# Second layer's entry in a two-layer decoder kernel: the overflow branch, three idle products, waits by depth half, and the bank of the first query projection

## The reference

```python
for i in range(DEPTH):
    if i % 2 == 0:
        mix = moba_attention(x, moba_w_in[j], moba_w_out[j], rel_bias)
    else:
        mix = nsa_attention(x, nsa_w_in[j], nsa_w_out[j], ..., rel_bias)
    x = layer_norm(DEEPNORM_ALPHA * x + mix, ln_g[i, 0], ln_b[i, 0])
    ffn = grouped_moe(x, router_w, router_b, moe_w_gate[i], moe_w_up[i], moe_w_down[i])
    x = layer_norm(DEEPNORM_ALPHA * x + ffn, ln_g[i, 1], ln_b[i, 1])

def nsa_attention(x, w_in, ...):
    proj = x @ w_in
    sizes = [H * d] + [Hkv * d] * 6 + [3 * H]
    q, kc, vc, ks, vs, kw, vw, g = jnp.split(proj, np.cumsum(sizes)[:-1].tolist(), axis=-1)
```

## Time and profile before

| | |
|---|---|
| median of 3 runs | 1209.3 us (1207.87 to 1209.31) |
| the profiled execution's own time | 1207.55 us |
| its span, first to last instruction | 1205.7 us |
| mean granted TensorE clock | 0.935 |
| PE busy | 1021.0 us, 85% of the span |
| DVE, ACT busy | 310.5 us, 183.4 us |
| chain that ended last | PE 52%, DMA 42%, DVE 2%, ACT 1%, issue 1% |
| HBM read | 446.72 MB |

### The profile page before, as it was taken

How to read it: one execution, slowest core, us unless ns; L and a number is a source line. 1 busy time by engine, 2 the same in 40 slices (tenths; PEclk the granted TensorE clock), 3 DMA queues, 4 the chain that set the end, 5 groups by cost and what they waited for, 6 DMA issues and landing times.

```text
span 1205.7 us, 18281 instructions
## 1 busy us (share of the span) xinstructions
PE 1021.0 (85%) x7610; PEld 565.5 (47%) x7610; DVE 310.5 (26%) x866; ACT 183.4 (15%) x473; POOL 43.3 (4%) x109
## 2 busy tenths in 40 slices
PE   9999999976698975668899999999967798876766
PEld 7586544443343532343678655544523433432432
DVE  2435521321111111111221785403211111111112
ACT  1024210110010000000221563201100010100002
POOL 1001010000000000000100120100000000000000
PEclk9999999998899988889999999999987899978888
DMA  9955899999999999999995308999999999999995
GB/s 354 364 210 192 341 373 418 427 427 427 427 428 428 426 425 429 428 428 422 368 352 214 137 1 316 357 422 425 426 427 428 426 426 428 428 426 428 427 426 236
DMA packets 56851, 449.05 MB, mean 372 GB/s; under 512 B 4643, under 2 KB 11044, under 8 KB 29628
## 3 DMA queue, kind: packets, MB, share of 16 engines
q1 hardware_dynamic: 54752, 442.52, 89.1%
q0 software_dynamic: 1680, 4.88, 1.1%
q10 hardware_dynamic: 332, 0.42, 0.1%
HBM read 446.72 MB, written 1.07 MB: 371 GB/s over the span
## 4 chain that ended last, share of the span: by engine, by line
PE 52%; DMA 42%; DVE 2%; ACT 1%; issue 1%; SPq 1%; DVEq 0%
DMA ring<-in_moe_w_down 16%; PE bank L1010 14%; DMA ring<-in_moe_w_up 11%; DMA ring<-in_moe_w_gate 10%; PE bank L779 7%; DMA bias<-in_moe_w_up 5%; PE bank L857 4%; PE bank L968 4%; PE bank L1074 3%; PE bank L1050 2%; PE bank L1224 2%; PE bank L1089 2%; PE bank L1331 1%; PE bank L1321 1%; PE bank L1061 1%; PE bank L1250 1%
## 5 line engine op out<-in xcount | busy, mean ns | idle before, releaser
L1010 PE MATMUL bank<-ring,work 128*32 128x256 f32 (+1 forms) x2656 | 323.6, 473 | 106.6 <-DMA ring<-in_moe_w_up 36.8
L1010 PEld LDWEIGHTS bank<-ring,work 128*32 128x32 f32 (+1 forms) x2656 | 151.9, 130 | 233.1 <-issue 201.8
L1635 DVE TENSOR_TENSOR work<-work,bank 128x256 f32<-128x256 f32 (+1 forms) x32 | 15.6, 487 | 526.0 <-PE bank L1010 526.0
L1074 PE MATMUL bank<-ring,work 128*32 128x512 f32 x576 | 99.3, 658 | 13.0 <-DMA ring<-in_moe_w_down 8.0
L1010 PE MATMUL bank<-softmax_area,work 128*32 128x256 f32 (+1 forms) x352 | 65.3, 499 | 32.8 <-DMA ring<-in_moe_w_gate 22.2
L779 PE MATMUL bank<-xT,ring 128*128 128x256 f32 x384 | 85.7, 382 | 1.1 <-ACT acc L482 1.1
L1648 DVE TENSOR_TENSOR xs<-xs,bank 128x512 f32<-128x512 f32 x112 | 71.0, 682 | 41.4 <-PE bank L1092 23.2
L779 PEld LDWEIGHTS bank<-xT,ring 128*128 128x128 f32 x384 | 72.1, 190 | 13.3 <-issue 3.8
L1010 PE MATMUL bank<-bias,work 128*32 128x256 f32 (+1 forms) x384 | 77.6, 485 | 0.0
L968 PE MATMUL bank<-work,acc 128*128 128x128 f32 (+1 forms) x448 | 75.5, 323 | 0.0
L968 PEld LDWEIGHTS bank<-work,acc 128*128 128x128 f32 x448 | 66.0, 191 | 16.6 <-issue 11.5
(11 more groups left out here) (286 smaller groups left out, 1128.3 us busy)
## 6 DMA issues: line engine op xcount, KB each, us to landing
ring<-in_moe_w_gate SPq DMA_DIRECT2D x44, 2048.0 KB, 28.7
ring<-in_moe_w_up SPq DMA_DIRECT2D x40, 2048.0 KB, 30.0
ring<-in_moe_w_down SPq DMA_DIRECT2D x36, 2048.0 KB, 29.2
softmax_area<-in_moe_w_down SPq DMA_DIRECT2D x8, 2048.0 KB, 25.8
bias<-in_moe_w_gate SPq DMA_DIRECT2D x6, 2048.0 KB, 33.1
softmax_area<-in_moe_w_up SPq DMA_DIRECT2D x6, 2048.0 KB, 28.5
bias<-in_moe_w_up SPq DMA_DIRECT2D x6, 2048.0 KB, 28.8
bias<-in_moe_w_down SPq DMA_DIRECT2D x6, 2048.0 KB, 33.3
```

The costliest lines, as they stand in the source:

```text
L1010: last = mm(bank[2 + k][row:row + cap, 0:width], xgT_of(group_of[i])[:, t, at + e * cap:at + (e + 1) * cap], w[e](t)[:, part * width:(part ...
L1074: last = mm(bank[5][row:row + CAP_NARROW, :], hidT_narrow[:, m, CAP_NARROW * e:CAP_NARROW * (e + 1)], w[e](m)[:, n * 512:(n + 1) * 512], s ...
```

## The change

Four edits, all at the second layer's entry. The four idle products at the end of `experts(0)` go; three stand instead behind `overflow(0)`, ahead of the wait for tile 0. `first_tiles` takes its products by depth half, each half with a wait of its own for the copy of that half; the wait for both halves goes. With it, a bank's start flag is set on its first product only, and its stop flag on its last. The first query projection (g = 3) is written to bank 5 and does not wait for bank 1, and ACT reads it there.

```diff
+        FIRST_QUERY_BANK = 5
...
             def project_T(l, g, w, lhs_cols, free=False):
 
+                b = FIRST_QUERY_BANK if l == 1 and g == 3 else g % 2
                 if not free:
                     proj_bank_free(l, g)
                 for n, pick_cols in enumerate(lhs_cols):
                     for t in range(KT):
-                        last = mm(bank[g % 2][:, n * SEQ:(n + 1) * SEQ], pick_cols(w, t), xT[:, t, :],
+                        last = mm(bank[b][:, n * SEQ:(n + 1) * SEQ], pick_cols(w, t), xT[:, t, :],
                                   start=(t == 0), stop=(t == KT - 1))
...
                 spread(l, PAIRS - 1)
-                if l + 1 < LAYERS:
-                    keep_warm(4)
...
-                    last = project_T(1, g, w, [tile_cols(2 * part), tile_cols(2 * part + 1)], free=(g == 4))
+                    last = project_T(1, g, w, [tile_cols(2 * part), tile_cols(2 * part + 1)], free=g in (3, 4))
...
             def first_tiles(tt, g):
                 w = nsa_slot(slot8, 0)
-                for n in range(2):
-                    for t in range(KT):
-                        last = mm(bank[g][:, n * SEQ + tt * P:n * SEQ + (tt + 1) * P], tile_cols(2 * g + n)(w, t),
-                                  xT[:, t, tt * P:(tt + 1) * P], start=(t == 0), stop=(t == KT - 1))
+                for half in range(2):
+                    pe.wait_ge(xT_copied, 2 * (2 * NT + tt) + half + 1)
+                    for n in range(2):
+                        for t in range(KT // 2 * half, KT // 2 * (half + 1)):
+                            last = mm(bank[g][:, n * SEQ + tt * P:n * SEQ + (tt + 1) * P], tile_cols(2 * g + n)(w, t),
+                                      xT[:, t, tt * P:(tt + 1) * P], start=tt == n == t == 0, stop=tt == n == 1 and t == KT - 1)
                 return last
 
+            keep_warm(3)
             normed(0, 1, 0)
             transpose_x(2, 0)
             arrived(1, 0)
-            xT_here(2, 0)
             first_tiles(0, 0)
             normed(0, 1, 1)
             transpose_x(2, 1)
             first_tiles(0, 1)
-            xT_here(2, 1)
...
-                    last = s_.mul(qT[:, 4 * c:4 * c + 2, :].rearrange("p m q -> p (m q)"), bank[1][:, :], DH ** -0.5)
+                    last = s_.mul(qT[:, 4 * c:4 * c + 2, :].rearrange("p m q -> p (m q)"), bank[FIRST_QUERY_BANK if g == 3 else 1][:, :], DH ** -0.5)
```

## The result

The changed kernel took 1211.51 us (median of 12 runs, 1209.51 to 1213.9), the kernel before 1209.37 us (12 runs, 1207.8 to 1211.89). The ratio is 1.0020, with a 95% interval of 1.0011 to 1.0029: slower by 1.3 to 3.5 us. The forecast was 1210.5 us in a range of 1207.1 to 1212.2.

A forecast was written before the change was run, and what follows sets the result against it. It took PE's work and waits between the layers as the bound, passed on one to one. +2.0 +1.3 -0.54 -0.45 -1.05 = +1.26, say +1.2 us, took 1209.3 to 1210.5 us; range 1207.1 to 1212.2.

The forecast's parts named there:

- my forecast proper: Second layer's entry: code fetched late, one spell of lower clock; +0.5 to +2.0 us, 1209.8 to 1211.3 us, chance 0.57.
- the slower rival: Behind layer 0's branch: code at 587.35 as now, two lower-clock spells; +3.4 us, 1212.7 us, chance 0.14.
- Code behind the branch: After layer 0's overflow branch: fetched code arrives at 586.7 us, the three products follow it, first transposes 2.0 us later.
- Clock: Behind 3.9 us of idle PE after the last expert sum: lower granted clock costs 1.3 us, bounds nothing and 2.74.
- Half waits: First projection of the second layer: starts after the first of two ACT copies, winning 0.54 us.
- Stall: Wait inside the first projection at 592.90 us: the second page of code comes in time, winning 0.45 us.
- Bank 5: First query projection: no longer waits for ACT's bank 1 copies, starts at 607.53 instead of 608.59 us, winning 1.05 us.
- Sum: Shift at the first query projection, passed on one to one: +2.0 +1.3 -0.54 -0.45 -1.05 = +1.26 us.
- the cheap branch: Layer 0's branch costs only 0.94 us: -2.5 to -2.95 us, 1206.4 to 1206.8 us; chance 0.17 for over 2.4 us gain.
- the kept clock: Rival behind layer 0's branch: fetch exposed but no clock loss, sum about -0.1 us, 1209.2 us, chance 0.12.

The follow-up runs named there:

- both_covers: The changed kernel with four idle products put back ahead of the branch, three kept behind it; 1209.91 us, ratio to the kernel before 1.0004.
- branch_only: The kernel before with only the idle products changed: none ahead of the overflow branch, three behind it; 1212.94 us, ratio 1.0033.
- halves_bank5: The changed kernel's depth-half waits and bank 5, with the four idle products ahead of the branch as before; 1208.84 us, ratio 0.9995.
- no_branch: halves_bank5 with TensorE's branch and overflow body of layer 0 left out; 1205.91 us, ratio to the kernel before 0.9978.

## Why the prediction came out as it did

The time lay in the range and on the forecast side, and the mechanism was the forecast one. Its size was too small: +1.26 us in the sum, +1.86 in the trace and +2.1 in the medians. The 1211.51 us lie just above the band of my forecast proper (1209.8 to 1211.3), toward the slower rival. By its steps:

- **Code behind the branch.** Right in kind: it is fetched, the products were its cover, and moved behind it they cover nothing. The size was off. I put the code at 586.7, 5.9 us after the spread's start, because I took the fetch to start sooner without products ahead of the branch. It did not: its packet started 3.7 us after the spread's start, as before. The code came at 6.46, and at 6.41 to 6.63 in every kernel whose branch stands behind the last spread. With the three products at the higher clock level that makes 2.58 us (4.28 less the clock's 1.70) where I had 2.0. Why that packet starts 3.7 us after the spread's start, and only 1.0 us after it at the end of layer 1 (1195.7 against 1194.71 in the earlier trace rows), no run shows. I put it down to the full transfer queues; that was not tested.
- **Clock.** Predicted 1.3, measured 1.70 (the changed kernel against both_covers); in branch_only 2.6 (5.28 against 2.68). The lower level came in all four kernels with 4.4 us and more of idle PE at this place. It lasted about 3.4 us in the changed kernel, but twice that in the other three (6.6 us and more at 0.50), in branch_only behind the same idle time of 4.47 us. So the single spell was in part luck: the length of the idle stretch, by which I had chosen it, does not decide it. With the 2.6 us of branch_only the sum would be +2.8 us. The upper value of "0.55 to 0.63" in the prediction stands in none of its rows.
- **Half waits.** Predicted 0.54; from the first transpose to the projection it is 1.36 us against 1.94, so 0.58. What I had not seen is a condition: where the first projection runs into the second piece of code, as in halves_bank5, the wait for that piece eats this gain.
- **Stall.** Predicted gone, 0.45 won. It is gone, and the block is 0.71 us shorter (3.65 against 4.36), which is more than the idle time of PE alone; before, the weight loads had stood still for 0.64 us there.
- **Bank 5.** Predicted 1.05, measured 1.13 (0.22 us from the start of L1350 to that of the query product, against 1.35).
- **Sum.** +4.28 -0.58 -0.71 -1.13 = +1.86 us at the query product. Both losses were larger than I had put them (by 0.58 and 0.40 us), and the three gains together by 0.38 us, so the errors partly cancel. Nothing behind the query product took it up or added to it beyond the noise: from its start to the span's end it is 597.1 us before and 597.3 after.

Of the rivals, the cheap branch is excluded by the 4.47 us of "issue" and the kept clock by PEclk. The slower one (code as late as now, two spells) was right on the code, and branch_only shows two spells. The changed kernel has a trace of one execution only; how many spells its other runs had, up to 1213.9 us, is not known.

## What to carry to other kernels

In this kernel a taken branch over a long body cost the engine a fetch, not a jump. Idle products that keep the clock belong ahead of such a branch; useful work should serve as well, which no run here tried. The time at which the fetched code arrives, not the last instruction's end, is what a step behind it waits for. A gap named "issue" a short way behind a branch can be the next piece of code: see whether a packet of the instruction queue starts 2.4 to 2.9 us ahead of the gap's end, as in these runs, and look where its edge lies before tuning waits in front of it, and move the edge by the length of the body that never runs. Where idle products are moved, ask what they cover besides the clock.

## What the runs showed of the hardware

- With the transfer engines busy (DMA share 1.04 to 1.07 in the changed kernel), code behind the taken branch arrived 6.41 to 6.63 us after the spread began, whether no or four idle products stood ahead of it. Where PE stopped for the next piece, it came 5.9 to 6.0 us after the first (the kernel before, halves_bank5, pad_short).
- The position of the stop follows the address: 35 transposes of padding moved it by 70 recorded instructions, 70 transposes removed it.
- The sequencer passes the branch while products ahead of it still wait to run: the first packet started 3.7 us after the spread's start both with four of them in front (584.5 us, the kernel before) and with none (585.6 us, the changed kernel). In no_branch there was no such packet.
- Behind 4.4 to 5.3 us of idle PE at this place the granted clock was 0.50 for a while in all four kernels that had such a stretch, and behind the same 4.47 us it was 0.50 for 3.4 us in one kernel and for 6.6 us and more in another.
